# High-part products first behind a norm, and four output tiles over six banks in the gated MLPs

## The chip, the core and the metric

The kernel runs on one core of a Trainium2 chip. The metric is device time in microseconds (us) from the start to the end of one execution; smaller is better. TensorE (PE) multiplies, with its weight loads in a row of their own (PEld); VectorE (DVE), ScalarE (ACT) and GpSimd (POOL) do the elementwise work; SyncE (SP) and ScalarE's queue issue the DMAs. PE adds up its products in eight banks of PSUM.

## What is computed

Two transformer blocks, one after the other, on 256 latent tokens and 256 context tokens of width 1024. The first block has two layers. Each begins and ends with a gated MLP at half weight behind a modulated norm, and has a mixer between them (gated delta rule in one layer, window attention in the other). The second block has a mixer of three branches, a cross attention and an MLP.

```python
def _modulated_norm(h, gain, shift, scale):
    return _rms_norm(h, gain) * (1.0 + scale) + shift

def _swiglu(h, w1, w2):
    a, b = jnp.split(h @ w1, 2, axis=-1)
    return (jax.nn.silu(a) * b) @ w2

for i in range(DEPTH):                       # 2 layers
    mx = (cond_x @ ada_w[i] + ada_b[i]).reshape(n_batch, 3, 3, 1, d)
...
    x = x + FFN_RESIDUAL * mx[:, 0, 2] * _swiglu(
        _modulated_norm(x, norm_g[i, 0], mx[:, 0, 0], mx[:, 0, 1]), ffn_w1[i, 0], ffn_w2[i, 0])
```

In the second block the norm is plain: the gated convolution begins with `rms_norm(h, norm_mix) @ w_in`, and the last MLP is `jnp.square(jax.nn.relu(u @ w_mlp_up)) @ w_mlp_down` with `u = rms_norm(h, norm_mlp)`.

## The kernel before

**Products.** Everything is kept with features on the partitions. A float32 operand is split into a high part (`hi`, rounded to the multiplier's format) and a low part (`lo`, the rest). The product of a weight tile of 128x128 with a token tile is three matmuls (`three`, L218): weights lo x tokens hi (L220), weights hi x tokens lo (L221), weights hi x tokens hi (L222). There are 512 tokens in the stages of mlp00, norm01 to norm11, and 256 in those behind norm12, norm mix and norm mlp. An output tile of 128 features takes eight depth steps (`KT` = 8), so 24 matmuls, in one bank.

**Weights.** They come in units of eight tiles (512 KB). SP loads a unit into one of three landing buffers and, for unit u, waits first for the low parts of unit u-3 (L2614). ACT makes the high parts in one of four slots, and waits for the landing and until PE has used unit u-4 (`feed_act`, L195). POOL makes the low parts (`feed_pool`, L207). Each engine has its order written out by hand; nothing is scheduled by a tool.

**A norm.** The row sums of the squares go through ACT (L411), DVE (L435) and PE (`spread_pe`, L417). Then, for each of the eight depth steps d, DVE multiplies (L441), ACT makes the high part of the normed tokens (L428, two halves where there are 512 tokens), DVE applies scale and shift again (L447) and POOL makes the low part (L463). DVE starts L447 of step d as soon as ACT has made the high part of d.

**`linear`** (L234) runs all products. The first `first` output tiles go side by side: for each d, PE waits for the low part of step d of the tokens (`ready(d)`), then does the three matmuls of each of these tiles. All other output tiles go one after the other, each through all eight d. Tile n is in bank n % 4, and `freed(n)` is the wait until its bank has been read. The gated MLPs' first half (`up_pe`) and the delta mixer's input (`delta_pe`) have first = 2, `glu_pe` and `mlp2_pe` have first = 4. `FIRST` (L2686) lays the weights out in the same order.

**Behind the products of the gated MLPs.** Even tiles are the gate (ACT's silu, L500), odd ones are multiplied with it by DVE (L515). At the start of each tile n, ACT runs `feed_act` up to the unit `max(n+1, first) + 3` of the stream, and only then waits for tile n.

**Work beside.** The modulation vectors of the later layers are computed while the first three gated MLPs (mlp00, mlp01, mlp10) and the delta mixer run, one block of the matrix `ada_w` (1 MB, into the one buffer `ada_landing`) for every two output tiles. ACT issues the first block's DMA behind the wait for tile 0, and PE uses it behind tile 2:

```python
def ada_beside_pe(k, pe, n, units):
    if n >= 2 and (n - 2) // 2 < len(units):
        (ada_turn_pe if n % 2 else ada_pe)(k, pe, units[(n - 2) // 2])

def ada_beside_act(k, act, n, units):
    if n == 0 and units:
        ada_dma(k, act, units[0])
    if n >= 2 and n % 2 == 0 and (n - 2) // 2 < len(units):
        u = units[(n - 2) // 2]
        ada_act(k, act, u)
        if u != units[-1]:
            ada_dma(k, act, u + 1)
```

`linear` calls `beside(n)` behind tile n; for the `first` tiles it calls it for all of them once they are all done.

Of the kernel before, what the change touches and what calls it, by code (L numbers as in the profile page):

```python
# [7 lines left out]
ACT = mybir.ActivationFunctionType  # L8
ALU = mybir.AluOpType
AX_X = mybir.AxisListType.X  # L10

P = 128
D = 1024
KT = D // P
CTX, LAT = 256, 256
# [215 lines left out]
    return k.WH[:, u % SLOTS, at:at + width], k.WL[:, u % SLOTS, at:at + width]  # L231


def linear(k, pe, st, stream, n_tiles, depth, x, tokens, freed, ready=None, first=1, beside=None):  # L234


    nc = k.nc

    def one(n, d):
        t = d * first + n if n < first else n * depth + d  # L240
        w = tile_parts(k, pe, stream, t)
        mm = three(nc, k.B[n % 4][:, 0:tokens], w, x(d), d == 0, d == depth - 1)
        names = []
        if t % UNIT == UNIT - 1:
            names.append(("unit used", k.F.unit(stream, t)))
        if d == depth - 1:
            names.append((st, "acc", n))
        if names:
            mm.then_inc(*k.PE.mark(*names))

    def begin(n):
        if freed(n) is not None:
            pe.wait_ge(*freed(n))

    for n in range(first):
        begin(n)
    for d in range(depth):
        if ready is not None and ready(d) is not None:
            pe.wait_ge(*ready(d))
        for n in range(first):  # L260
            one(n, d)
    for n in range(first):
        if beside is not None:
            beside(n)
    for n in range(first, n_tiles):
        begin(n)
        for d in range(depth):
            one(n, d)
        if beside is not None:
            beside(n)  # L270
# [205 lines left out]

def up_freed(k, st):
    return lambda n: None if n < 4 else (k.DV.after(st, "raw", (n - 4) // 2) if n % 2 else k.AC.after(st, "silu", (n - 4) // 2))  # L480


def up_pe(k, pe, st, stream, x, tokens, ready, units=(), extra=None):
    def beside(n):
        ada_beside_pe(k, pe, n, units)
        if extra is not None:
            extra(n)
    linear(k, pe, st, stream, 2 * FT, KT, x, tokens, up_freed(k, st), ready, first=2, beside=beside)


def up_act(k, act, st, stream, tokens, hi, units=(), extra=None):
    nc = k.nc
    for n in range(2 * FT):
        p = n // 2
        feed_act(k, act, k.F.ahead(stream, max(n + 1, 2) * KT))
        if n % 2 == 0:
            act.wait_ge(*k.PE.after(st, "acc", n))
            if p >= 2:
                act.wait_ge(*k.DV.after(st, "lo", p - 2))
            nc.scalar.activation(k.sil[:, p % 2, 0:tokens], k.B[n % 4][:, 0:tokens], ACT.Silu).then_inc(*k.AC.mark((st, "silu", p)))  # L500
        else:
            act.wait_ge(*k.DV.after(st, "raw", p))
            nc.scalar.activation(hi(p), k.sil[:, p % 2, 0:tokens], ACT.Copy).then_inc(*k.AC.mark((st, "hi", p)))  # L503
        ada_beside_act(k, act, n, units)
        if extra is not None:
            extra(n)


def up_dve(k, dve, st, tokens, hi, lo, units=(), extra=None):
    nc = k.nc  # L510
    for p in range(FT):
        s = k.sil[:, p % 2, 0:tokens]
        dve.wait_ge(*k.PE.after(st, "acc", 2 * p + 1))
        dve.wait_ge(*k.AC.after(st, "silu", p))
        nc.vector.tensor_tensor(s, s, k.B[(2 * p + 1) % 4][:, 0:tokens], ALU.mult).then_inc(*k.DV.mark((st, "raw", p)))  # L515
        dve.wait_ge(*k.AC.after(st, "hi", p))
        nc.vector.tensor_tensor(lo(p), s, hi(p).bitcast(F32), ALU.subtract).then_inc(*k.DV.mark((st, "lo", p)))  # L517
        for n in (2 * p, 2 * p + 1):
            ada_beside_dve(k, dve, n, units)
        if extra is not None:  # L520
            extra(p)
# [6 lines left out]
def down_freed(k, up, st):  # L528
    def freed(n):
        if n >= 4:  # L530
            return k.DV.after(st, "ev", n - 4)
        return k.DV.after(up, "raw", FT - 2 + n // 2) if n % 2 else k.AC.after(up, "silu", FT - 2 + n // 2)
    return freed


# [61 lines left out]
def delta_pe(k, pe):  # L597

    nc, st = k.nc, "dn"

    def freed(n):
        if n < 4:
            return None
        m = n - 4
        return k.AC.after(st, "abt") if m == 0 else k.DV.after(st, "conv", m - 1) if m <= QKV else k.AC.after(st, "z", m - 1 - QKV)

    def beside(n):
        m = n - 3
        if 0 <= m < 16:
            pe.wait_ge(*k.AC.after(st, "sq", m))  # L610
            for c in range(CHUNKS):
                mm = nc.tensor.matmul(k.B[4][:, m * 4 + c:m * 4 + c + 1], k.sq[:, m % 2, c * P:(c + 1) * P], k.C["ones"][:, 0:1],
                                      start=m == 0 and c == 0, stop=True, skip_group_check=True)
            mm.then_inc(*k.PE.mark((st, "stat", m)))
        ada_beside_pe(k, pe, n, ADA_DELTA)
        if n == 2:
            pe.wait_ge(*k.AC.after(st, "abt"))
            for c in range(CHUNKS):
                mm = nc.tensor.transpose(k.B[5][:, c * 32:(c + 1) * 32], k.abt[0:32, c * P:(c + 1) * P], k.C["ident"][0:32, 0:32])
            mm.then_inc(*k.PE.mark((st, "ab")))  # L620
        if n == 5:
            pe.wait_ge(*k.DV.after(st, "g"))
            for d in range(2):
                g = k.dg["g"][:].rearrange("p (c d h) -> p c d h", d=2, h=8)[:, :, d, :]
                nc.tensor.matmul(k.B[5][:, 128 + d * 32:160 + d * 32], k.C["until"][:, d, :], g, start=True, stop=True)
                mm = nc.tensor.matmul(k.B[5][:, 192 + d * 32:224 + d * 32], k.C["ones"], g, start=True, stop=True)
            mm.then_inc(*k.PE.mark((st, "sums")))
        if n > QKV:
            if n == QKV + 1:
                pe.wait_ge(*k.DV.after(st, "r"))  # L630
            for m in (2 * (n - QKV - 1), 2 * (n - QKV - 1) + 1):
                m = m // 2 + 8 * (m % 2)
                bank = 5 + m // 8
                if m % 8:
                    pe.wait_ge(*k.DV.after(st, "normed", m - 1))
                for c in range(CHUNKS):
                    mm = nc.tensor.transpose(ck(k.B[bank], c), column(k.rr, m * 4 + c).to_broadcast([P, P]), k.C["ident"])
                mm.then_inc(*k.PE.mark((st, "spread", m)))

    linear(k, pe, st, "w_dn", DN_TILES, KT, lambda d: (k.n_hi[:, d, :], k.n_lo[:, d, :]), TOK, freed,  # L640
           lambda d: k.PO.after("norm01", "lo", d), first=2, beside=beside)


def delta_act(k, act):
# [855 lines left out]
def both2(k):  # L1500
    return lambda d: (k.m_hi[:, d, :], k.m_lo[:, d, :])
# [35 lines left out]

def glu_pe(k, pe):
    freed = lambda n: None if n < 4 else k.AC.after("glu", "sig", (n - 4) // 2) if n % 2 else k.DV.after("glu", "ev", (n - 4) // 2)
    linear(k, pe, "glu", "w_glu", 2 * KT, KT, both2(k), LAT, freed, lambda d: k.PO.after("norm mix", "lo", d), first=4)  # L1540


def glu_act(k, act):
# [747 lines left out]

def mlp2_pe(k, pe):
    freed = lambda n: k.DV.after("up2", "square", n - 4) if n >= 4 else None
    linear(k, pe, "up2", "w_mlp_up", 4 * KT, KT, both2(k), LAT, freed, lambda d: k.PO.after("norm mlp", "lo", d), first=4)
    out_pe(k, pe, "down2", "w_mlp_down", 4 * KT, lambda d: (k.mh_hi[:, d, :], k.mh_lo[:, d, :]), LAT,
           lambda n: k.DV.after("down2", "ev", n - 4) if n >= 4 else k.DV.after("up2", "square", 4 * KT - 4 + n),
           lambda d: k.DV.after("up2", "lo", max(d, 4 * KT - 5)) if d == 0 or d > 4 * KT - 5 else None)
# [63 lines left out]
def mlp_pe(k, pe, st, extra=None):  # L2361
    norm, up, down, l, n, tokens, after, units = MLPS[st]
    a = TOK - tokens
    hi, lo = hidden(k, tokens)
    up_pe(k, pe, st, "w_" + up, lambda d: (k.n_hi[:, d, a:TOK], k.n_lo[:, d, a:TOK]), tokens, lambda d: k.PO.after(norm, "lo", d), units, extra)
    out_pe(k, pe, st + " down", "w_" + down, FT, lambda d: (hi(d), lo(d)), tokens, down_freed(k, st, st + " down"), down_ready(k, st), stat=after)


# [290 lines left out]
def build(nc, dram, out, steps, counted):  # L2659
    with ExitStack() as ctx:  # L2660
        k = Kit(nc, ctx, dram, steps, counted)
        with nc.Block() as block:
# [21 lines left out]


FIRST = {"w_dn": 2, "w_dn_out": 4, "w_swa_k": 2, "w_swa_out": 4, "w_glu": 4, "w_k": 2, "w_ssd_out": 4,  # L2686
         "w_mix": 4, "w_xo": 4, "w_mlp_up": 4, "w_up00": 2, "w_up01": 2, "w_up10": 2, "w_up11": 2}


def pack(t, name, w):  # L2690
# [158 lines left out]
```

## Time and profile before

| | |
|---|---|
| median of 3 runs | 3163.7 us (3160.8 to 3165.36) |
| the profiled execution, its own time | 3158.29 us |
| its span, first to last instruction | 3156.2 us |
| PE busy | 2999.3 us, 95% of the span |
| mean granted TensorE clock | 0.970 |

The span and all rows below are of one profiled execution. A row of the timeline gives the start in us from the span's start, the duration, the engine, the source line, the operation, what it writes and reads, and, in brackets, how long the engine sat idle before it and who ended that. Matmuls overlap, so the duration of one is longer than the step from one start to the next.

### The profile page before, as it was taken

The page shows a single profiled execution, that of the slowest core. Times are in us where ns is not written, and L with a number is a line of the kernel's source. Part 1 is how long each engine was busy: PE and PEld are TensorE (multiplying, and loading weights), DVE is VectorE, ACT ScalarE, POOL GpSimd, SP SyncE. Part 2 cuts the span into 40 slices and gives each one's busy share as a digit, 9 for nine tenths or more (in the row PEclk, how much of TensorE's full clock was granted, in tenths as well). Part 3 has the DMA queues.
Part 4 walks back from the last instruction along what each step waited for, and adds up shares of the span by engine and source line. Part 5 has one row for each costly group of instructions (what it writes and reads, how often), then busy time and mean ns, then how long its engine had stood idle before and what let it go on. Part 6 is the DMA issues. An engine that isn't in the chain of part 4 may idle for free.

```text
span 3156.2 us, 47130 instructions
## 1 busy us (share of the span) xinstructions
PE 2999.3 (95%) x19462; PEld 2584.0 (82%) x19462; DVE 1244.8 (39%) x2298; ACT 1248.1 (40%) x2122; POOL 1617.3 (51%) x810
## 2 busy tenths in 40 slices
PE   8999999989999899999999999899999898998899
PEld 5777878779999777777777888589999698997899
DVE  2222135524444422211322114745335776622570
ACT  3222234335555332222322224454445556544453
POOL 4333443344443443344433445168887276596587
PEclk9999999999999999999999999899999899998999
DMA  6544224310000144432454323435545153354255
GB/s 251 176 167 148 94 94 156 109 47 1 1 1 1 47 168 178 161 107 94 142 178 135 105 92 88 82 115 189 185 155 176 45 169 112 108 168 140 94 188 167
DMA packets 96884, 381.45 MB, mean 121 GB/s; under 512 B 10369, under 2 KB 15649, under 8 KB 87201
## 3 DMA queue, kind: packets, MB, share of 16 engines
q1 hardware_dynamic: 87456, 311.33, 30.5%
q10 hardware_dynamic: 9216, 67.11, 6.2%
q8 instruction: 155, 2.54, 0.3%
q14 instruction: 57, 0.46, 0.0%
HBM read 374.21 MB, written 4.19 MB: 120 GB/s over the span
## 4 chain that ended last, share of the span: by engine, by line
PE 85%; DVE 5%; POOL 4%; ACT 3%; issue 1%; DMA 1%; SPq 0%; ACTq 0%; POOLq 0%; DVEq 0%
PE bank L220 23%; PE bank L221 22%; PE bank L222 22%; PE bank L750 5%; PE bank L293 2%; POOL weights_lo L213 2%; PE bank L1388 1%; DVE norm_work L447 1%; PE bank L769 1%; DVE norm_work L441 1%; DVE square_sums L405 1%; ACT dn_xt L1036 1%; PE bank L375 1%; ACT weights_hi L203 0%; PE bank L847 0%
## 5 line engine op out<-in xcount | busy, mean ns | idle before, releaser
L213 POOL TENSOR_TENSOR weights_lo<-weights_landing,weights_hi 128x1024 fp32r<-128x1024 f32 x554 | 1334.8, 2413 | 1192.7 <-ACT weights_hi L203 1191.7
L203 ACT ACTIVATE weights_hi<-weights_landing 128x1024 fp32r<-128x1024 f32 x554 | 586.5, 1060 | 1319.6 <-PE bank L222 1238.6
L220 PE MATMUL bank<-normed_hi,weights_lo 128*128 128x256 f32 (+1 forms) x2864 | 979.6, 342 | 39.5 <-POOL normed_lo L463 23.3
L221 PE MATMUL bank<-normed_lo,weights_hi 128*128 128x256 f32 (+1 forms) x2864 | 963.5, 336 | 0.0
L222 PE MATMUL bank<-normed_hi,weights_hi 128*128 128x256 f32 (+1 forms) x2864 | 962.3, 336 | 0.0
L220 PEld LDWEIGHTS bank<-normed_hi,weights_lo 128*128 128x128 f32 x2864 | 546.3, 191 | 133.2 <-issue 32.3
L222 PEld LDWEIGHTS bank<-normed_hi,weights_hi 128*128 128x128 f32 x2864 | 545.6, 190 | 61.5
L221 PEld LDWEIGHTS bank<-normed_lo,weights_hi 128*128 128x128 f32 x2864 | 546.5, 191 | 56.3
L221 PE MATMUL bank<-hidden_lo,weights_hi 128*128 128x512 f32 (+1 forms) x960 | 329.3, 343 | 0.0
L222 PE MATMUL bank<-hidden_hi,weights_hi 128*128 128x512 f32 (+1 forms) x960 | 329.3, 343 | 0.0
L220 PE MATMUL bank<-hidden_hi,weights_lo 128*128 128x512 f32 (+1 forms) x960 | 329.3, 343 | 0.0
L515 DVE TENSOR_TENSOR silus<-silus,bank 128x512 f32<-128x512 f32 (+1 forms) x88 | 54.7, 621 | 565.1 <-PE bank L222 540.1
L517 DVE TENSOR_TENSOR hidden_lo<-silus,hidden_hi 128x512 fp32r<-128x512 f32 (+1 forms) x88 | 212.5, 2415 | 89.6 <-ACT hidden_hi L503 89.6
L222 PEld LDWEIGHTS bank<-hidden_hi,weights_hi 128*128 128x128 f32 x960 | 180.2, 188 | 24.4
L220 PEld LDWEIGHTS bank<-hidden_hi,weights_lo 128*128 128x128 f32 x960 | 180.2, 188 | 24.2
L221 PEld LDWEIGHTS bank<-hidden_lo,weights_hi 128*128 128x128 f32 x960 | 180.2, 188 | 24.1
L944 POOL TENSOR_TENSOR dn_lm<-dn_at,dn_level 128x512 f32<-128x512 f32 (+1 forms) x96 | 114.8, 1212 | 159.7 <-PE bank L750 159.5
L572 DVE SCALAR_TENSOR_TENSOR residual<-bank,gate,residual 128x256 f32<-128x256 f32 x80 | 35.5, 479 | 376.6 <-PE bank L222 376.6
L463 POOL TENSOR_TENSOR normed_lo<-norm_work,normed_hi 128x512 fp32r<-128x512 f32 (+1 forms) x72 | 76.4, 1065 | 82.6 <-DVE norm_work L447 82.6
L1100 DVE TENSOR_TENSOR dn_y<-dn_y,bank 128x512 f32<-128x512 f32 (+1 forms) x96 | 61.7, 643 | 107.2 <-PE bank L750 96.2
L1522 DVE SCALAR_TENSOR_TENSOR bank<-gl,k_pack,bank 128x255 f32<-128x255 f32 (+14 forms) x210 | 99.3, 473 | 7.4
L750 PE MATMUL bank<-dn_xt,dn_lm 128*128 128x128 f32 x640 | 84.1, 285 | 12.2 <-ACT dn_xt L1036 11.3
(414 smaller groups left out, 3906.0 us busy)
## 6 DMA issues: line engine op xcount, KB each, us to landing
weights_landing<-w_up SPq DMA_DIRECT2D x176, 512.0 KB, 3.5
ada_landing<-w_ada ACTq DMA_DIRECT2D x64, 1024.0 KB, 4.9
weights_landing<-w_down SPq DMA_DIRECT2D x88, 512.0 KB, 3.5
weights_landing<-w_dn SPq DMA_DIRECT2D x33, 512.0 KB, 3.5
weights_landing<-w_mlp_up SPq DMA_DIRECT2D x32, 512.0 KB, 3.5
weights_landing<-w_mlp_down SPq DMA_DIRECT2D x32, 512.0 KB, 3.6
weights_landing<-w_gate SPq DMA_DIRECT2D x24, 512.0 KB, 4.3
weights_landing<-w_xbc SPq DMA_DIRECT2D x24, 512.0 KB, 3.5
```

The source lines that it names most:

```text
L203: k.nc.scalar.activation(k.WH[:, u % SLOTS, :], k.W[:, u % LANDS, :], ACT.Copy).then_inc(*k.AC.mark(("unit hi", u)))
L213: k.nc.gpsimd.tensor_tensor(k.WL[:, u % SLOTS, :], k.W[:, u % LANDS, :], k.WH[:, u % SLOTS, :].bitcast(F32), ALU.subtract).then_inc(*k.PO. ...
L220: nc.tensor.matmul(out, ll, rh, start=start, stop=False, skip_group_check=True)
L221: nc.tensor.matmul(out, lh, rl, start=False, stop=False, skip_group_check=True)
L222: return nc.tensor.matmul(out, lh, rh, start=False, stop=stop, skip_group_check=True)
L293: mm = nc.tensor.matmul(k.B[6][32 * j:32 * j + 32, 0:256], k.cond32[:, u % 4 * 2 + d, :], k.ada[slot][:, (d * 4 + j) * 256:(d * 4 + j + 1) ...
L463: k.nc.gpsimd.tensor_tensor(lo(d), work(d), hi(d).bitcast(F32), ALU.subtract).then_inc(*k.PO.mark((st, "lo", d)))
L517: nc.vector.tensor_tensor(lo(p), s, hi(p).bitcast(F32), ALU.subtract).then_inc(*k.DV.mark((st, "lo", p)))
L750: mm = k.nc.tensor.matmul(ck(bank, c), lhs[:, c, :], rhs[:, c, :], start=True, stop=True)
L944: nc.gpsimd.tensor_tensor(k.lm[d][part], k.at_[d][part], level_mask(k, d, s)[part], ALU.mult).then_inc(*k.PO.mark(("head", i, "lm", s, d)))
L1100: nc.vector.tensor_tensor(y, y, bank, ALU.subtract).then_inc(*k.DV.mark(("head", i, "y", s, d)))
L1522: nc.vector.scalar_tensor_tensor(y[:, a:LAT], x[:, 0:LAT - a], w[:, at, j:j + 1], y[:, a:LAT], ALU.mult, ALU.add).then_inc(*k.DV.mark(("co ...
```

## The change

`linear` gets two parameters. With `high`, each depth step of the tiles side by side is cut in two: PE waits for the **high** part of the tokens (made by ACT) and does for each tile the two matmuls that need only it (L271 and L272 of the new code); then it waits for the low part (made by POOL) and does the third matmul of each tile (`low_part`, L242). With `banks`, tile n is in bank n % banks.

`high` is given behind norm00, norm01, norm02, norm10, norm12, norm mix and norm mlp; norm11 and norm xattn stay as they were. In the four gated MLPs first goes from 2 to 4 and the banks from 4 to 6. The calls of `beside` are not edited.

```diff
-def linear(k, pe, st, stream, n_tiles, depth, x, tokens, freed, ready=None, first=1, beside=None):
+def linear(k, pe, st, stream, n_tiles, depth, x, tokens, freed, ready=None, first=1, beside=None, banks=4, high=None):
...
+    def low_part(n, d):
+        t = d * first + n
+        u, at = k.F.unit(stream, t), t % UNIT * P
+        mm = nc.tensor.matmul(k.B[n][:, 0:tokens], k.WH[:, u % SLOTS, at:at + P], x(d)[1], start=False, stop=d == depth - 1,
+                              skip_group_check=True)
+        done(mm, t, n, d)
...
     for d in range(depth):
+        if high is not None:
+            pe.wait_ge(*high(d))
+            for n in range(first):
+                (wh, wl), (xh, xl) = tile_parts(k, pe, stream, d * first + n), x(d)
+                nc.tensor.matmul(k.B[n][:, 0:tokens], wl, xh, start=d == 0, stop=False, skip_group_check=True)
+                nc.tensor.matmul(k.B[n][:, 0:tokens], wh, xh, start=False, stop=False, skip_group_check=True)
+            pe.wait_ge(*ready(d))
+            for n in range(first):
+                low_part(n, d)
+            continue
...
+UP_BANKS = 6
...
 def up_freed(k, st):
-    return lambda n: None if n < 4 else (k.DV.after(st, "raw", (n - 4) // 2) if n % 2 else k.AC.after(st, "silu", (n - 4) // 2))
...
+    return lambda n: (None if n < UP_BANKS else k.DV.after(st, "raw", (n - UP_BANKS) // 2) if n % 2 else
+                      k.AC.after(st, "silu", (n - UP_BANKS) // 2))
...
-    linear(k, pe, st, stream, 2 * FT, KT, x, tokens, up_freed(k, st), ready, first=2, beside=beside)
+    linear(k, pe, st, stream, 2 * FT, KT, x, tokens, up_freed(k, st), ready, first=4, beside=beside, banks=UP_BANKS, high=high)
...
-        feed_act(k, act, k.F.ahead(stream, max(n + 1, 2) * KT))
+        feed_act(k, act, k.F.ahead(stream, max(n + 1, 4) * KT))
...
     linear(k, pe, st, "w_dn", DN_TILES, KT, lambda d: (k.n_hi[:, d, :], k.n_lo[:, d, :]), TOK, freed,
-           lambda d: k.PO.after("norm01", "lo", d), first=2, beside=beside)
+           lambda d: k.PO.after("norm01", "lo", d), first=2, beside=beside, high=lambda d: k.AC.after("norm01", "hi", d))
```

`glu_pe` and `mlp2_pe` get `high` in the same way, the banks in `up_act`, `up_dve` and `down_freed` follow `UP_BANKS`, and `FIRST` has 4 for the four streams of the MLPs.

**PE at the start of mlp00, before.** The first row is the last of the modulation before the MLP, then the tokens' step d = 0 for output tiles 0 and 1.

```order
L307 MATMUL bank7<-k_cond_pack,ada_pieces_66 128x8 x2
L220 MATMUL bank0<-normed_hi_49,weights_lo 128x512
L221 MATMUL bank0<-normed_lo_50,weights_hi 128x512
L222 MATMUL bank0<-normed_hi_49,weights_hi 128x512
L220 MATMUL bank1<-normed_hi_49,weights_lo 128x512
L221 MATMUL bank1<-normed_lo_50,weights_hi 128x512
L222 MATMUL bank1<-normed_hi_49,weights_hi 128x512
```

The same place, changed:

```order
L271 MATMUL bank0<-normed_hi_49,weights_lo 128x512
L272 MATMUL bank0<-normed_hi_49,weights_hi 128x512
L271 MATMUL bank1<-normed_hi_49,weights_lo 128x512
L272 MATMUL bank1<-normed_hi_49,weights_hi 128x512
...
L271 MATMUL bank3<-normed_hi_49,weights_lo 128x512
L272 MATMUL bank3<-normed_hi_49,weights_hi 128x512
L242 MATMUL bank0<-normed_lo_50,weights_hi 128x512
L242 MATMUL bank1<-normed_lo_50,weights_hi 128x512
```

The second matmul needed the tokens' low part; now eight matmuls stand before the first that does, over four banks.

**PE around the first block of ada_w in mlp00, before**, behind output tile 2 (bank 2) and ahead of tile 3:

```order
L221 MATMUL bank2<-normed_lo_50,weights_hi 128x512
L222 MATMUL bank2<-normed_hi_49,weights_hi 128x512
L293 MATMUL bank6<-ada_landing_65,cond32 32x256 x8
L220 MATMUL bank3<-normed_hi_49,weights_lo 128x512
L221 MATMUL bank3<-normed_lo_50,weights_hi 128x512
```

Changed:

```order
L242 MATMUL bank2<-normed_lo_50,weights_hi 128x512
L242 MATMUL bank3<-normed_lo_50,weights_hi 128x512
L312 MATMUL bank6<-ada_landing_65,cond32 32x256 x8
L220 MATMUL bank4<-normed_hi_49,weights_lo 128x512
L221 MATMUL bank4<-normed_lo_50,weights_hi 128x512
```

The block stood behind the whole of tile 2, 24 matmuls after the end of tiles 0 and 1; it now stands right behind the last matmuls of tiles 0 to 3, and ahead of tile 4.

**ACT at the same place, before** (the tokens' high parts, then units of weights, then the gate of tile 0 and the DMA of the block):

```order
L428 ACTIVATE normed_hi_49<-norm_work_51,mod,scale 128x256 x16
L203 ACTIVATE weights_hi<-weights_landing 128x1024 x3
L500 ACT_TABLE_LOAD
L500 ACTIVATE silus_55<-bank0 128x512
L282 DMA ada_landing_65<-w_ada 128x2048
```

Changed:

```order
L203 ACTIVATE weights_hi<-weights_landing 128x1024 x5
L523 ACT_TABLE_LOAD
L523 ACTIVATE silus_55<-bank0 128x512
L301 DMA ada_landing_65<-w_ada 128x2048
L526 ACTIVATE hidden_hi_52<-silus_55 128x512
```

The DMA keeps its place behind tile 0's wait, with two more units of weights ahead of it.

## Rows read from the trace of the kernel before

**Rows 1.** The page: busy us of PE, share of the span, instructions.
```profile
PE 2999.3 (95%) x19462; PEld 2584.0 (82%) x19462; DVE 1244.8 (39%) x2298; ACT 1248.1 (40%) x2122; POOL 1617.3 (51%) x810
```

**Rows 2.** Waits of PE: us in total, times, longest us.
```profile
PE bank L220 <- POOL normed_lo L463: 23.3, 9, 4.0
...
PE bank L220 <- DVE gl L1556: 5.4, 1, 5.4
...
PE bank L220 <- issue: 4.1, 1, 4.1
...
PE bank L220 <- DVE relu_squares L2330: 2.9, 1, 2.9
```

**Rows 3.** Timeline of norm02 and the start of mlp01.
```profile
1097.13 0.74 DVE L447 TENSOR_SCALAR norm_work<-norm_work,scale,mod 128x256 f32<-128x256 f32 x2
...
1099.27 0.80 PE L220 MATMUL bank<-normed_hi,weights_lo 128*128 128x512 f32 x1 [4.03 <-POOL normed_lo L463]
...
1111.63 7.12 POOL L213 TENSOR_TENSOR weights_lo<-weights_landing,weights_hi 128x1024 fp32r<-128x1024 f32 x3
```

**Rows 4.** Timeline, the same step of norm00 and norm10.
```profile
40.30 0.73 DVE L447 TENSOR_SCALAR norm_work<-norm_work,scale,mod 128x256 f32<-128x256 f32 x2 [1.16 <-ACT normed_hi L428]
...
42.43 0.80 PE L220 MATMUL bank<-normed_hi,weights_lo 128*128 128x512 f32 x1 [3.71 <-POOL normed_lo L463]
...
1503.71 0.73 DVE L447 TENSOR_SCALAR norm_work<-norm_work,scale,mod 128x256 f32<-128x256 f32 x2
...
1505.85 0.80 PE L220 MATMUL bank<-normed_hi,weights_lo 128*128 128x512 f32 x1 [4.02 <-POOL normed_lo L463]
```

**Rows 5.** Stretches (PE): us, busy us (instructions), granted clock, DMA share, GB/s.
```profile
41.90:45.30 3.40, 2.87 (x7) 0.51 0.00 0
...
1120.00:1131.20 11.20, 11.20 (x48) 1.00 0.61 209
2306.40:2311.80 5.40, 5.39 (x25) 0.50 0.38 131
2968.10:2974.00 5.90, 5.83 (x27) 0.50 0.01 1
2982.40:2985.20 2.80, 0.00 (x0) 1.00 0.70 203
```

**Rows 6.** Timeline, first blocks of ada_w on PE in mlp00, mlp01 and mlp10.
```profile
61.21 1.07 PE L293 MATMUL bank<-ada_landing,cond 128*32 128x256 f32 x16
...
1118.91 1.07 PE L293 MATMUL bank<-ada_landing,cond 128*32 128x256 f32 x16
...
1525.52 1.07 PE L293 MATMUL bank<-ada_landing,cond 128*32 128x256 f32 x16
```

**Rows 7.** Tile ada_landing: landing of all 64 DMAs, of those issued at 1113.56, 1120.05.
```profile
DMA to landing us min/median/max: 4.6/4.9/7.8
...
DMA to landing us min/median/max: 4.8/4.8/4.8
...
DMA to landing us min/median/max: 7.5/7.5/7.5
```

**Rows 8.** Timeline, the last low part behind norm01, and PE.
```profile
459.26 1.28 POOL L463 TENSOR_TENSOR normed_lo<-norm_work,normed_hi 128x512 fp32r<-128x512 f32 x1 [0.23 <-DVE norm_work L447]
...
460.60 0.50 PE L220 MATMUL bank<-normed_hi,weights_lo 128*128 128x512 f32 x1
```

**Rows 9.** Timeline, norm12 and the start of mlp11.
```profile
2093.59 0.41 DVE L447 TENSOR_SCALAR norm_work<-norm_work,scale,mod 128x256 f32<-128x256 f32 x1
...
2094.87 0.58 PE L220 MATMUL bank<-normed_hi,weights_lo 128*128 128x256 f32 x1 [2.40 <-POOL normed_lo L463]
...
2104.31 1.28 ACT L500 ACT_TABLE_LOAD   x1
...
2109.94 1.06 ACT L203 ACTIVATE weights_hi<-weights_landing 128x1024 fp32r<-128x1024 f32 x1 [1.60 <-DMA weights_landing<-w_up]
```

**Rows 10.** Timeline, the gated convolution's first tiles.
```profile
2303.15 1.06 ACT L203 ACTIVATE weights_hi<-weights_landing 128x1024 fp32r<-128x1024 f32 x1 [1.75 <-DMA weights_landing<-w_glu]
```

## What the change should do to the time

> **What bounds the kernel now.** I read the page first: PE is busy for 95% of the span [rows 1], so a change pays only where PE stands still or runs at half clock, or where it makes PE do either. Then the waits of PE, sorted by what ended them: 23.3 us in nine waits for the tokens' low parts, 4.1 us of the same kind put down to "issue", 5.4 and 2.9 us for the readers of a bank in the two stages that already had four tiles side by side [rows 2]. Then the timeline around each norm, and the granted clock there. The whole prize of this change is in the first class, some 27 us, of which the part from high to low can go.
>
> **Part 1: the start behind a norm, 512 tokens.** DVE starts L447 of step 0 when the high part of step 0 is made, so its start is the moment at which the changed PE may begin. In mlp01 that is 1097.13, and PE began at 1099.27 [rows 3]: 2.1 us. In mlp00 it is 40.30 against 42.43, in mlp10 1503.71 against 1505.85 [rows 4]: 2.1 us each. The later steps should not hold it: 48 matmuls take 11.2 us [rows 5], 0.233 us each, so a depth step of four tiles is 12 x 0.233 = 2.8 us. The low part of step 7 is ready at 1111.6, when POOL goes on to weights [rows 3]; seven steps after step 0's at 1099.2 make it 1.8 us a step. PE is now the slower one.
>
> The fourth unit of weights is needed at depth step 6 and is made behind the norm's low parts: the first of three at 7.12/3 = 2.4 us from 1111.63 [rows 3], so at 1114.0. PE reaches step 6 at 1097.1 + 72 x 0.233 + the half-clock surcharge of about 2 us = 1115.9. Covered, by 1.9 us.
>
> **Part 2: the clock.** Behind each of these fronts PE runs at half clock at first: 2.9 us in mlp00 (42.43 to 45.3), 5.8 in the last MLP, and 5.4 behind the bank wait in the gated convolution; these are the first, the last and one of the middle of eight such stretches with a mean of 4.3 us [rows 5]. Each costs half of its length: 2.15 us on the mean. Beginning 2.1 us earlier should on the mean let the clock rise 2.1 us earlier; I count no change, with 1.1 us per front as the bound to the bad side (it rises when it did, and the early time is spent at half clock). In mlp00 PE would stand still for only 1.6 us (to 40.3, from 42.43 - 3.71 = 38.7 [rows 4]), so the clock may not fall there: I take half of the surcharge of 1.45 us, 0.7.
>
> **Part 3: the block of ada_w loses its cover.** ACT issues the first block's DMA behind the wait for tile 0; PE's order has the block behind tile 2. Before, tile 0 ended with tile 1 and the whole of tile 2 (24 x 0.233 = 5.6 us) lay between: the DMA issued at 1113.56 took 4.8 us [rows 7], and PE took the block at 1118.91 [rows 6]. That cover had 0.5 us to spare. Now tile 0 ends together with tiles 2 and 3, and nothing lies between. Queued behind the waiting block on PE are tile 4 and all that follows. The DMA landed in 4.8 us there; the next one, issued at 1120.05 while units of weights were still coming in, took 7.5 us [rows 7]. The new one is issued at about 1121.7, beside the tail of the same units; I take 5.9 us, nearer to the lower end because most of those units have landed by then, and keep 4.8 and 7.5 as ends.
>
> The three stages, from the first product to the end of "four tiles and one block":
> - mlp01, before: 1118.91 + 1.0 for the block + 5.7 for tile 3 = 1125.6 (26.3 us from the first product; 22.4 of products, 1.0 of block and 2.15 of clock leave 0.8 lost to later steps). Now: 1097.2 + 96 x 0.233 (22.4) + 2.15 = 1121.75; + 0.15 (issue) + 5.9 + 0.1, then 1.0 for the block = 1128.9. **3.3 us later.**
> - mlp10, before: 1525.52 + 6.7 = 1532.2. Now: 1503.8 + 22.4 + 2.15 = 1528.35, + 7.15 = 1535.5. **3.3 us later.**
> - mlp00, before: 61.21 + 6.7 = 67.9. Now: 40.4 + 22.4 + 0.7 + 0.2 (step 0's low part) = 63.7, + 7.15 = 70.8. **2.9 us later.**
>
> Together 9.5 us; with landings of 4.8 us 6.2, with 7.5 us 14.3.
>
> The Trainium skill ("DMA: Bandwidth & Descriptors", section "Queues, rings and completion order") says that each DMA engine takes turns between the queues that have work. By that alone a 1 MB block beside a 512 KB unit would always be the late one, and the upper end, 14.3 us, would be the term and the sum +18.7 instead of +13.9. The rows show both 4.8 and 7.5 us, so they do not settle it.
>
> **Part 4: the clock behind the new stall.** PE stands still for about 6.1 us in each of the three stages. The trace has two idle stretches of this kind between dense products: 5.4 us in the gated convolution, after which PE ran at 0.50 for 5.4 us, and 2.9 us in the last MLP, where the clock stayed at 1.00 [rows 2, 5]. The new ones are longer than the first, so I let the clock fall in all three, at the mean surcharge: 3 x 2.15 = 6.4 us (bounds: 0, and 3 x 2.7 = 8.1).
>
> On this the Trainium skill ("TensorE: Matmul & The Clock Gate", section "Loop structure matters more than you think") speaks against the change: a wait for a DMA between bursts of products drops the array to half rate. The trace agrees at 5.4 us of idling and not at 2.9. With the rule the term is 6.4 us, without it 0 and the sum +7.5.
>
> **Part 5: the delta mixer.** Here two tiles stay side by side, and tile 2 still covers the block. POOL ended the last low part at 460.54 and PE went on at 460.60 [rows 8]; six matmuls followed (1.4 us + 0.1), now two (0.5). The steps before it have the same pace of POOL. Gain 1.0 us; no less than 0.9, no more than the 2.1 of the other fronts.
>
> **Part 6: the stages with 256 tokens.** In mlp11 PE may begin at 2093.6 instead of 2094.87 [rows 9]: 1.3 us. But the gate of tile 0 stands on ACT behind the eighth unit, which landed at 2109.94 [rows 9] behind POOL's and SP's chain, not PE's; with the 1.06 us of that unit, a table load of 1.28 and the gate itself it frees bank 0 at 2112.3 at the earliest. Six banks let PE do tiles 4 and 5 meanwhile. The gain is the 1.3 us or, where the clock rises when it did, half of that; I take 1.0 (bounds 0.6 and 1.3). In the gated convolution the same chain (eighth unit at 2303.15 [rows 10]) ends PE's wait of 5.4 us, with four banks before and after: PE arrives earlier and waits longer. **0.** The last MLP has this form too, with its wait of 2.9 us [rows 2]: 0, but the wait grows to some 4 us, and if the clock then falls, up to 2.7 us are lost.
>
> **Nothing for the rest.** The number of matmuls and weight loads is the same. Four or six banks gain nothing in the steady part, where 48 matmuls fill 11.2 us without a gap [rows 5]. The down products' first banks are read 15 us before they are needed, or 0.6 us behind tile 42, with tile 43's 5.6 us as cover.
>
> **Sum.** 9.5 + 6.4 - 1.0 - 1.0 = +13.9 us. On the profiled execution: 3158.3 + 13.9 = 3172.2 us. It stands 5.4 us below the median of 3163.7; the sum carries over to the median: **3177.6 us**, 0.4% slower.
>
> **The rivals.**
> - **Faster.** The block's wait costs nothing: the mechanism would be that the DMA lands under PE's products after all. Then the fronts are left: 3 x 2.1, 3 x 0.8 of later steps and 0.7 of clock in mlp00, with 2.0 from parts 5 and 6: -11 us, 3153 us. For it: 27 us of waits of PE [rows 2]. Against: the DMA stands behind tile 0 on ACT in the listing, and tile 0 cannot end before the last depth step. It decides from a DMA time below 1 us; the least of 64 is 4.6 [rows 7]. Chance 0.06.
> - **The stall, but the clock holds and the DMA lands in about 4.8 us.** 6.2 - 2.0 = +4, 3168 us, within what can't be told from no change. For it: the idle stretch of 2.9 us kept the clock, and half of the 64 blocks landed within 4.9 us [rows 7]. Against: 5.0 us of idling is near the 5.4 after which it fell. Chance 0.22.
> - **Slower still.** The second block, issued behind the first one's products, has only tile 4 before it (5.6 us): it waits where its DMA takes more than that (the one of 7.5 us did), about 1 us in each stage, and the last MLP's wait lets the clock fall: 14.3 + 8.1 + 2.7 - 2.0 = +23, 3187 us; the waits of the second blocks are inside this bound, since a stalled clock gives them cover. Chance 0.14.
> - The forecast, 0.58: 3171 to 3183.
>
> **Range and chances.** A measurement of this kernel can tell about 0.2% (6.3 us) from no change. From the cases: faster 0.06; same 0.18 (most of the second rival, and a little of the forecast); slower 0.76. The range reaches down into the second rival and up to the third: 3166 to 3187 us.
>
> **What would show it.** In the changed profile: PE waits for "DMA ada_landing" three times for 5 to 8 us, in mlp00, mlp01 and mlp10, and no other stage has it; PE's wait for normed_lo is gone but for the delta mixer, and in its place stand waits of some 2 us for ACT's normed_hi; the wait for L1556's line grows by 1 us or more; clock 0.50 behind the three stalls. The step most open to error is the clock: where in its course the stalls fall can't be read from the trace of before. I am wrong if the DMA is issued before tile 0 ends, or if PE does other products while it waits.

## The result

| | changed | before, in the same comparison |
|---|---|---|
| median | 3181.5 us (3176.8 to 3185.6) | 3162.8 us (3160.8 to 3165.4) |
| profiled execution | 3176.8 us | 3158.3 us |
| its span, mean clock | 3174.8 us, 0.970 | 3156.2 us, 0.970 |

The ratio is 1.006, with an interval from 1.0045 to 1.0076: 18.8 us slower, 18.5 us on the profiled executions. The forecast was +13.9 us, slower. Direction and mechanism hold, the size is 5 us short.

The page of the changed kernel: the span, and the busy us, share and instructions of each engine. The counts of instructions are those of before [rows 1].

```profile
span 3174.8 us, 47130 instructions
...
PE 3001.1 (95%) x19462; PEld 2585.0 (81%) x19462; DVE 1236.8 (39%) x2298; ACT 1247.3 (39%) x2122; POOL 1616.8 (51%) x810
```

PE is busy for only 1.8 us longer, so most of the difference is standing still. Half clock counts as busy time; what the new waits add of it is about made up for in other stretches, since the mean clock is 0.970 in both profiled executions. The waits of PE in the changed kernel (us in total, times, longest us):

```profile
PE bank L312 <- DMA ada_landing<-w_ada: 23.0, 3, 8.9
...
PE bank L271 <- ACT normed_hi L447: 8.7, 6, 1.9
...
PE bank L220 <- DVE gl L1580: 4.9, 1, 4.9
...
PE bank L220 <- DVE relu_squares L2354: 4.6, 1, 4.6
...
PE bank L220 <- POOL normed_lo L482: 4.0, 1, 4.0
...
PE bank L271 <- issue: 2.0, 1, 2.0
```

Set against [rows 2]: the waits for low parts, 23.3 us in nine and 4.1 us of "issue", have shrunk to one of 4.0 (norm11, which was not changed) and one of 0.3 in the delta mixer. In their place stand 8.7 us for high parts and 2.0 of "issue", the same wait in the delta mixer. So the change took 12.4 us of waiting from the fronts (27.4 less 15.0). A wait that was not there before gives back 23.0 us: three times PE stands before the block of ada_w. Its half-clock tail comes on top.

The timeline of mlp01 in the changed kernel, from the first product to the second block. SPq and ACTq rows are DMA issues; in brackets stands how long the engine was idle before, and for whom.

```profile
1102.38 0.80 PE L271 MATMUL bank<-normed_hi,weights_lo 128*128 128x512 f32 x1 [1.91 <-ACT normed_hi L447]
...
1124.03 2.68 SPq L2640 DMA_DIRECT2D weights_landing<-w_up  x2
...
1126.34 1.10 PE L242 MATMUL bank<-normed_lo,weights_hi 128*128 128x512 f32 x4
...
1127.53 1.06 ACT L203 ACTIVATE weights_hi<-weights_landing 128x1024 fp32r<-128x1024 f32 x1 [3.69 <-PE bank L242]
1127.61 0.33 ACTq L301 DMA_DIRECT2D ada_landing<-w_ada  x1
...
1134.71 1.94 PE L312 MATMUL bank<-ada_landing,cond 128*32 128x256 f32 x16 [7.28 <-DMA ada_landing<-w_ada]
...
1136.71 0.33 ACTq L301 DMA_DIRECT2D ada_landing<-w_ada  x1
...
1143.18 1.07 PE L312 MATMUL bank<-ada_landing,cond 128*32 128x256 f32 x16
```

Before, PE came from tile 2 straight to its block at 1118.91 [rows 6]. Now its last product of the four tiles is in the row of 1126.34. It ends at 1127.44, ACT issues the DMA at 1127.61, and PE's next product is at 1134.71. SP had issued two units of weights at 1124.03 and 1126.38, just ahead of the block, and another followed at 1131.00. The block's 16 matmuls take 1.94 us instead of 1.07: they run at half clock. The second block does not wait.

How long the three first blocks took from issue to landing, in mlp00, mlp01 and mlp10 of the changed kernel:

```profile
DMA to landing us min/median/max: 8.7/8.7/8.7
...
DMA to landing us min/median/max: 7.1/7.1/7.1
...
DMA to landing us min/median/max: 6.5/6.5/6.5
```

Stretches of PE in the changed kernel (us, busy us and instructions, granted clock, DMA share, GB/s): the front of mlp00, the front of mlp01, behind the stalls of mlp00, mlp01 and mlp10, and in the last MLP:

```profile
40.60:43.60 3.00, 2.91 (x11) 1.00 0.00 0
1102.30:1107.60 5.30, 5.22 (x12) 0.50 0.01 3
72.50:76.80 4.30, 4.26 (x22) 0.50 0.32 84
1134.70:1138.40 3.70, 3.69 (x20) 0.50 0.38 83
1547.20:1551.40 4.20, 4.12 (x21) 0.50 0.31 80
3002.10:3005.50 3.40, 3.06 (x14) 0.50 0.75 183
```

The same marks in the two profiled executions give this account, in us:

| stage | forecast | measured |
|---|---|---|
| mlp00 | 2.9 + 2.15 = +5.0 | +7.7 |
| delta mixer | -1.0 | -0.9 |
| mlp01 | 3.3 + 2.15 = +5.4 | +6.6 |
| mlp10 | 3.3 + 2.15 = +5.4 | +6.2 |
| mlp11 | -1.0 | -1.1 |
| gated convolution to the cross attention | 0 | +1.1 |
| last MLP | 0, up to 2.7 lost | +0.9 |
| all others together | 0 | -2.0 |
| sum | +13.9 | +18.5 |

The last three rows before the sum cancel by chance (+1.1, +0.9, -2.0), so the 4.6 us that the forecast lacks stand in the three MLPs with a block.

### The profile page after: what moved, and what is told of

It is laid out like the page before. It is cut to its first block, busy times and chain, and to the rows that moved or that the text cites. A ratio compares the mean times of both kernels' runs of the same rounds, so it can differ in the third digit from the quotient of the medians.

```text
span 3174.8 us, 47130 instructions
## 1 busy us (share of the span) xinstructions
PE 3001.1 (95%) x19462; PEld 2585.0 (81%) x19462; DVE 1236.8 (39%) x2298; ACT 1247.3 (39%) x2122; POOL 1616.8 (51%) x810
## 4 chain that ended last, share of the span: by engine, by line
PE 85%; DVE 5%; POOL 4%; ACT 3%; DMA 2%; issue 1%; SPq 0%; ACTq 0%; POOLq 0%; DVEq 0%
PE bank L220 22%; PE bank L221 21%; PE bank L222 21%; PE bank L774 5%; PE bank L312 2%; POOL weights_lo L213 2%; PE bank L1412 1%; PE bank L793 1%; PE bank L242 1%; PE bank L271 1%; PE bank L272 1%; DVE square_sums L424 1%; DMA ada_landing<-w_ada 1%; DVE norm_work L466 1%; ACT dn_xt L1060 1%
## 5 line engine op out<-in xcount | busy, mean ns | idle before, releaser
L220 PE MATMUL bank<-normed_hi,weights_lo 128*128 128x256 f32 (+1 forms) x2656 | 903.0, 340 | 17.6 <-DVE gl L1580 4.9
L221 PE MATMUL bank<-normed_lo,weights_hi 128*128 128x256 f32 (+1 forms) x2656 | 888.9, 335 | 0.0
L222 PE MATMUL bank<-normed_hi,weights_hi 128*128 128x256 f32 (+1 forms) x2656 | 887.6, 334 | 0.0
L220 PEld LDWEIGHTS bank<-normed_hi,weights_lo 128*128 128x128 f32 x2656 | 503.5, 190 | 101.4 <-issue 29.3
L222 PEld LDWEIGHTS bank<-normed_hi,weights_hi 128*128 128x128 f32 x2656 | 503.1, 189 | 56.1
L221 PEld LDWEIGHTS bank<-normed_lo,weights_hi 128*128 128x128 f32 x2656 | 504.1, 190 | 51.7
L540 DVE TENSOR_TENSOR hidden_lo<-silus,hidden_hi 128x512 fp32r<-128x512 f32 (+1 forms) x88 | 198.2, 2252 | 110.5 <-ACT hidden_hi L526 110.5
```

The lines of the kernel that those rows point to most:

```text
L220: nc.tensor.matmul(out, ll, rh, start=start, stop=False, skip_group_check=True)
L221: nc.tensor.matmul(out, lh, rl, start=False, stop=False, skip_group_check=True)
L222: return nc.tensor.matmul(out, lh, rh, start=False, stop=stop, skip_group_check=True)
```

## The experiments

The theory: the stall exists because the DMA of the first block is issued behind tile 0, and it lasts as long as that DMA. The rivals: four tiles over six banks, or the products with high parts, are themselves the cost; or the DMA is late because of the units of weights beside it, and its place does not matter. "Before" was timed again beside each: 3161.2 us beside the first four, 3162.7 us beside the others.

**Issue the DMA ahead of tile 0.** ACT issues the first block at the head of the stage; PE's order is untouched.

```diff
 def ada_beside_act(k, act, n, units):
-    if n == 0 and units:
+    if n == 0 and units and units is ADA_DELTA:
         ada_dma(k, act, units[0])
...
     nc = k.nc
+    if units:
+        ada_dma(k, act, units[0])
     for n in range(2 * FT):
```

> The changed kernel, with the DMA of the first block of ada_w in each of the three gated MLPs issued by ACT ahead of the weights' high parts and ahead of the wait for tile 0, so that it lands under the four tiles. PE's order is that of the change. My theory (the block's lost cover and the half clock behind it are the whole loss): PE's three waits for this DMA (8.9, 7.3 and 6.7 us) go, and the 5.9 us of clock with them. The second block has only tile 4 before it, so 0 to 2 us of wait may stand there in each stage. 3181.5 - 22.9 - 5.9 + 2 = 3155 us (3151 to 3160), faster than the kernel before by 3 to 11 us. Rival (the order of the products, two and then one matmul to a bank, costs PE its pace): the waits go too, but the time stays above 3165 us, and 96 matmuls of a front take visibly more than 22.4 us at full clock.

Measured: 3164.9 us (3160.4 to 3173.0), ratio to before 1.0008 (0.9998 to 1.0018). That is above the expected range and can't be told from before. Some 15 us are back and the place of the DMA is confirmed as the cause of most of the loss, but the 6 us of gain that were forecast are missing. PE waits no more for the first block, but now for the second. The waits of PE, the timeline of mlp01 on PE and ACT, and a stretch of PE behind the wait, of this kernel:

```profile
PE bank L312 <- DMA ada_landing<-w_ada: 9.7, 3, 3.9
...
1122.79 1.07 PE L312 MATMUL bank<-ada_landing,cond 128*32 128x256 f32 x16
1125.33 0.60 ACT L525 ACTIVATE silus<-bank 128x512 f32<-128x512 f32 x1
1126.75 0.63 ACT L528 ACTIVATE hidden_hi<-silus 128x512 fp32r<-128x512 f32 x1 [0.82 <-DVE silus L540]
1126.76 0.33 ACTq L301 DMA_DIRECT2D ada_landing<-w_ada  x1
...
1132.49 1.07 PE L312 MATMUL bank<-ada_landing,cond 128*32 128x256 f32 x16 [2.86 <-DMA ada_landing<-w_ada]
...
1133.90:1137.20 3.30, 3.30 (x9) 0.50 0.93 328
```

PE does the first block at 1122.79, and the second block's DMA, which only has to wait for that, leaves at 1126.76: 4.0 us later. It stands in ACT's queue behind a unit of weights, the table load and gate of tile 0, and hidden_hi, which waits for DVE. Between the blocks lie tile 4 and nothing else. Three waits of 3.9, 2.9 and 2.9 us and 3.4 us at half clock soon after each use up the gain: 9.7 + 3 x 1.7 = 15 us.

**High parts first, nothing else.** Two tiles side by side and four banks, as before.

```diff
-UP_BANKS = 6
+UP_BANKS = 4
...
-    linear(k, pe, st, stream, 2 * FT, KT, x, tokens, up_freed(k, st), ready, first=4, beside=beside, banks=UP_BANKS, high=high)
+    linear(k, pe, st, stream, 2 * FT, KT, x, tokens, up_freed(k, st), ready, first=2, beside=beside, banks=UP_BANKS, high=high)
...
-        feed_act(k, act, k.F.ahead(stream, max(n + 1, 4) * KT))
+        feed_act(k, act, k.F.ahead(stream, max(n + 1, 2) * KT))
```

> The high parts first, as in the change, but two tiles side by side over four banks in the gated MLPs, as before. My theory: each norm with 512 tokens saves the four matmuls that no longer follow the last low part, 1.0 us as in the delta mixer, and mlp11 0.5 us; no wait for a block of ada_w. 3162.8 - 4.5 = 3158 us (3155 to 3161). Rival (the new order of products costs by itself): no faster than before, above 3165 us.

Measured: 3158.3 us (3153.8 to 3164.2), ratio 0.9991 (0.9978 to 1.0003): the median is as expected, and the interval takes in no change. Each front with 512 tokens begins 2.1 us earlier; mlp00 ends 0.8 us earlier, mlp01 0.9, and mlp10, where half clock held on longer, 0.4. With two tiles PE catches up with POOL in the last depth steps, and what is kept are at best the four matmuls less behind the last low part, 4 x 0.233 = 0.93 us.

**Four tiles and six banks, low parts in their old place.**

```diff
-        if high is not None:
+        if False:
```

> Four tiles over six banks in the gated MLPs, as in the change, but each depth step waits for the low part first and does its three matmuls tile by tile, everywhere. My theory: the waits for the blocks of ada_w stay, 5 to 9 us each, the fronts begin 2.1 us later with 512 tokens and 1.3 with 256. 3181.5 + 3 x 1.5 + 1.0 + 1.0 = 3188 us (3184 to 3192). Rival (high parts first is what costs): faster than the changed kernel, below 3178 us.

Measured: 3182.9 us (3179.6 to 3184.5), ratio 1.006 (1.0045 to 1.0075), 1 us below the expected range. It is as slow as the whole change: without the high parts first, the fronts end later, and the block waits shorter. The waits of PE:

```profile
PE bank L220 <- POOL normed_lo L482: 23.0, 8, 4.0
...
PE bank L312 <- DMA ada_landing<-w_ada: 18.1, 3, 7.2
...
PE bank L220 <- issue: 4.1, 1, 4.1
```

PE waits 12 us longer for the tokens than in the changed kernel (23.0 and 4.1 of "issue", against 8.7, 4.0, 2.0 of "issue" and 0.3), but 4.9 us less for the block, which lands in 4.9, 7.0 and 5.5 us: where the fronts end later, less comes in beside its DMA. The profiled executions, the slowest run of this kernel and the fastest of the changed one, lie 7.7 us apart, the medians 1.3 us. The whole loss against before comes with four tiles side by side.

**Early block, four banks.** The first experiment with `UP_BANKS = 4`.

> The changed kernel with the first block's DMA issued early, as in the run before, and four banks in place of six. My theory: tile 4 now waits until ACT has read tile 0, which stands behind the eighth unit of weights (1.06 us), a table load (1.28) and the gate (0.6): 2.0 to 2.4 us of wait behind the block in each of the three stages, and some 5 us in mlp11, where clock is lost too. 11 us above the run with early block and six banks, about 3166 us. Rival (six banks do nothing): the same time as with six.

Measured: 3170.8 us (3164.9 to 3176.8), ratio 1.0028 (1.0014 to 1.0041): 5.9 us over the first experiment where 11 were expected. The waits of PE, and PE behind the four tiles of mlp01:

```profile
PE bank L220 <- ACT silus L525: 12.5, 4, 6.2
...
1123.81 0.50 PE L220 MATMUL bank<-normed_hi,weights_lo 128*128 128x512 f32 x1 [2.12 <-ACT silus L525]
```

Four banks leave tile 4 without a bank for 2.1 us with 512 tokens and 6.2 us in mlp11, so the two further banks are what saves mlp11. In the other stages the 2.1 us cost nothing net: they lie between the two blocks and cover the second block's DMA, whose waits go down from 9.7 us to one of 1.8. In the two profiled executions four banks make mlp11 some 7 us longer and the three stages with a block 5.3 us shorter; that the medians lie further apart than this stays open.

**The block in the middle of the four tiles.** PE takes the first block behind depth step 4 (`mid`) and the second where the first one stood. ACT issues both ahead of tile 0, and its issue at tile 0 is left to the delta mixer.

```diff
             for n in range(first):
                 low_part(n, d)
+            if mid is not None and d == 4:
+                mid()
             continue
...
-    if n >= 2 and (n - 2) // 2 < len(units):
+    if n >= (2 if units is ADA_DELTA else 4) and (n - 2) // 2 < len(units):
         (ada_turn_pe if n % 2 else ada_pe)(k, pe, units[(n - 2) // 2])
...
+    if units:
+        ada_dma(k, act, units[0])
+        feed_act(k, act, k.F.ahead(stream, 2 * KT))
+        ada_act(k, act, units[0])
+        ada_dma(k, act, units[1])
     for n in range(2 * FT):
```

> The changed kernel with cover for the first two blocks of ada_w of each gated MLP: ACT issues the first block's DMA ahead of the weights, PE multiplies it behind depth step 4 of the four tiles, and ACT issues the second block's DMA right then, some 14 us before PE needs it behind tile 4. My theory (lost cover is the whole loss): no wait for ada_landing in the MLPs and no half clock behind the fronts' ends; each of the three MLPs then ends 2.9 us earlier than in the kernel before, the delta mixer saves 0.9 and mlp11 1.2 us, the last MLP loses up to 2 us by its longer wait. 3161 - 10 = 3151 us (3148 to 3156). Rival (four tiles with high parts first bring nothing of themselves, the gain is taken back elsewhere): within 3 us of the kernel before.

Measured: 3152.5 us (3149.2 to 3159.9), ratio 0.9978 (0.9966 to 0.9991), as expected. PE in mlp01 (and the DMA issue of the second block):

```profile
1107.70 1.07 PE L314 MATMUL bank<-ada_landing,cond 128*32 128x256 f32 x16
1108.84 0.34 ACTq L303 DMA_DIRECT2D ada_landing<-w_ada  x1
...
1122.89 1.07 PE L314 MATMUL bank<-ada_landing,cond 128*32 128x256 f32 x16
```

No wait for ada_landing is left: 14 us lie between issue and use. Against before, mlp00 is 3.7 us faster, mlp01 2.0, mlp10 2.6. This is what the fronts are worth once they cost no cover: 8.3 us, where the faster rival had set 9.4 (three times 2.1 and 0.8, and 0.7).

**Only the cover taken away from the kernel before.** Nothing of the change is in it: the block stands ahead of tile 2 instead of behind it.

```diff
+    if units and units is not ADA_DELTA and n == 1:
+        ada_pe(k, pe, units[0])
-    if n >= 2 and (n - 2) // 2 < len(units):
+    if n >= 2 and not (units is not ADA_DELTA and n == 2) and (n - 2) // 2 < len(units):
```

> The kernel before, with one thing moved: in the three gated MLPs PE takes the first block of ada_w right behind tiles 0 and 1 instead of behind tile 2. Nothing else of the change is in it. My theory: three waits for the block, of 5.1 us each since here the units of weights are issued behind the block and not ahead of it (it landed in 4.8 to 5.0 us in the kernel before), and half clock behind most of them: +15 and +4 to 6 us, 3181 us (3176 to 3184). Rival (the change's loss comes from four tiles or from the new order of the products): well below 3172 us, since neither is here.

Measured: 3181.7 us (3181.4 to 3182.0), ratio 1.0068 (1.0048 to 1.0088), as expected. The same loss as the whole change, by itself. The waits of PE, the stall in mlp01, and the clock behind it:

```profile
PE bank L293 <- DMA ada_landing<-w_ada: 16.2, 3, 5.9
...
1124.59 1.93 PE L293 MATMUL bank<-ada_landing,cond 128*32 128x256 f32 x16 [5.07 <-DMA ada_landing<-w_ada]
...
1124.50:1129.60 5.10, 5.01 (x23) 0.50 0.64 250
```

That the loss equals that of the whole change is a coincidence of size: it has no gain at the fronts, and shorter waits. Here the DMAs land in 5.7, 4.8 and 5.0 us, each with a unit of weights issued 0.3 to 0.5 us behind it. From the first product of the front on, the three stages are 8.6, 7.5 and 7.1 us longer: the wait (5.9, 5.1, 5.2) and 1.9 to 2.7 us more, mostly half clock. So my 5.9 us is more than enough for a DMA without units just ahead of it, and the changed kernel's landings are longer for another reason.

**The units of weights held back.** The changed kernel, but SP issues the ninth unit of each of the three streams only when PE is through with the first block.

```diff
         if u >= LANDS:
             sp.wait_ge(*k.PO.after("unit lo", u - LANDS))
+        if u in held:
+            sp.wait_ge(*k.PE.after("ada acc", held[u]))
         sp.dma_start(k.W[:, u % LANDS, :], F.source[u]).then_inc(k.landed[u % LANDS], 16)
```

> The changed kernel with SP's loads from the ninth unit of each of the three MLPs' weights on held back until PE has used the first block of ada_w. My theory (the block's DMA took 8.7, 7.1 and 6.5 us because units of weights were under way ahead of it and beside it): it lands in about 4.8 us in all three, PE's waits fall from 22.9 to about 15.5 us in total, and 3181.5 - 7.5 = 3174 us. Rival (a DMA on ACT's queue is slow after the queue's long rest): landings as before, and no gain.

Measured: 3175.5 us (3170.5 to 3178.2), ratio 1.0045 (1.0027 to 1.0063): 6 us below the changed kernel where 7.5 were expected. The waits, the block of mlp01 and the landing of its DMA:

```profile
PE bank L312 <- DMA ada_landing<-w_ada: 15.3, 3, 5.2
...
1131.21 1.93 PE L312 MATMUL bank<-ada_landing,cond 128*32 128x256 f32 x16 [5.00 <-DMA ada_landing<-w_ada]
...
DMA to landing us min/median/max: 4.8/4.8/4.8
```

With the units gone the block lands in 5.0, 4.8 and 4.9 us instead of 8.7, 7.1 and 6.5. PE's waits fall by 7.7 us, which covers the 4.7 that the forecast lacked (it had allowed 5.9 us for a landing). A queue that is slow after a rest is ruled out with it. The rest, a stall of 5 us and the fallen clock, stays: the place of the issue is the first cause, the units beside it the second.

**Six banks in the gated convolution and the last MLP too**, on top of the block in the middle.

```diff
-    freed = lambda n: None if n < 4 else k.AC.after("glu", "sig", (n - 4) // 2) if n % 2 else k.DV.after("glu", "ev", (n - 4) // 2)
+    freed = lambda n: None if n < 6 else k.AC.after("glu", "sig", (n - 6) // 2) if n % 2 else k.DV.after("glu", "ev", (n - 6) // 2)
...
-    freed = lambda n: k.DV.after("up2", "square", n - 4) if n >= 4 else None
+    freed = lambda n: k.DV.after("up2", "square", n - 6) if n >= 6 else None
```

`banks=6` goes to both calls of `linear`, and the readers of the banks take n % 6.

> The run with the block in the middle, and six banks also in the gated convolution and the last MLP's first half. My theory: there the first reader of a bank stands behind the eighth unit's landing, and PE's waits of 5 and 4.6 us for it shrink by the 5.6 us that tiles 4 and 5 take, with the half clock behind them (2.7 and 1.7 us): 9 to 13 us less than the run with the block in the middle, about 3140 us. Rival (what is saved there is waited for at the next unit, since POOL and the landings set the pace): no more than 4 us less.

Measured: 3136.8 us (3134.4 to 3138.9), ratio to before 0.9928 (0.9904 to 0.9952), 15.7 us below the version with the block in the middle, where 9 to 13 were expected. With four banks PE stood still for 6.1 and 4.6 us in that version; here the waits for gl and relu_squares are gone, and these are stretches of PE in the gated convolution and the last MLP:

```profile
2290.00:2297.00 7.00, 7.00 (x62) 1.00 0.63 213
...
2970.00:2975.00 5.00, 5.00 (x45) 1.00 0.46 156
```

PE does tiles 4 and 5 where it used to wait, and the clock does not fall behind: 7.7 us in the convolution and 6.2 us in the last MLP, more than the waits by the half clock behind them. This kernel beats both, by 26 us against before and 45 against the change.

## Why the prediction was right, and where it was short

- **Part 1, the fronts: right.** PE's first product comes 2.1 us earlier against its surroundings in all three (mlp00 at 40.67, forecast 40.4). The four tiles of mlp00 end at 63.60, forecast 63.7; in mlp01 and mlp10 they take 25.05 and 24.9 us from the first product, forecast 24.55. The difference is the clock.
- **Part 2, the clock of the fronts: near, in part by luck.** mlp01's front ran for 5.3 us at half clock where the mean of 4.3 was taken. In mlp00 the clock did not fall at all, where half a surcharge was set. But behind the same 1.60 us of idling it fell there in the profile with the units held back, and PE ran at 0.50 for 6.1 us.
- **Part 3, the block: right in kind, too small. This is the term that was mis-sized.** PE waits three times for ada_landing and nowhere else, as told. The term took a landing of 5.9 us, "nearer to the lower end because most of those units have landed by then". They had not. In mlp01 and mlp10 two units left in the 3.6 us ahead of the block and another 3.4 us behind it; in mlp00 one left 2.3 us ahead and one 0.1 us behind. Landings were 8.7, 7.1 and 6.5 us, with a mean of 7.4, and mlp00's is above the upper end of 7.5. The waits add up to 23.0 us where 18.3 were forecast (three of 6.1): 4.7 us, as much as the sum lacks. The Trainium skill ("DMA: Bandwidth & Descriptors", section "Queues, rings and completion order"), by which each engine takes turns between the queues that have work, gave +18.7; the measured +18.5 and the landings of 5.0 us or less once the units are held back agree with it. The nearness of the sum is in part luck: the 7.5 us put to it was one landing of before, and mlp10's was 6.5. That a block beside a unit is always the late one does not hold here: six times, in the kernel before and in the one that lost only the cover, a unit was issued 0.3 to 0.5 us behind a first block. The block landed in 4.8 to 5.7 us, and the unit took 5.6 to 6.1 instead of some 3.5. The late blocks were those with units just ahead of them, and the one with a unit 0.1 us behind.
- **Part 4, the clock behind the stalls: right.** It fell in all three, for 4.3, 3.7 and 4.2 us with PE at work: about half of that, 6 us, was lost, forecast 6.4. The rule of the Trainium skill ("TensorE: Matmul & The Clock Gate", section "Loop structure matters more than you think") holds here: behind idle stretches of 4.6 to 8.9 us PE ran at 0.50 each time. The length of the wait alone does not decide below that. The 2.9 us after which the clock stayed at 1.00 were no bound: it fell soon after two waits of 2.9 us in the first experiment and at two of the three waits of 2.1 us in the fourth, whose last MLP kept it behind 3.6 us. What decides there is open.
- **Part 5, the delta mixer: right.** 0.9 us of gain, forecast 1.0; the high-part experiment shows that it is the four matmuls.
- **Part 6: mlp11 right** (1.1 us, forecast 1.0). In the last MLP the wait grew from 2.9 to 4.6 us and the clock fell behind it, the bound that was named; it cost 0.9 us net, and up to 2.7 were allowed for. The convolution's wait did not grow, as "what would show it" had it: 4.9 us against 5.4. It goes with the clock of that front: 6.0 us at half clock in the changed kernel and 3.3 before. With 3.3 us and the block in the middle it was 6.1, with 3.1 us in the high-part experiment 6.2, so at the same clock it does grow, by 0.7 to 0.8 us. Why the stretch to the cross attention is 1.1 us longer I did not settle.
- **The other signs.** The three waits were told as 5 to 8 us, and mlp00's was 8.9. The wait for normed_lo that is left is norm11's, which the forecast had passed over, and not the delta mixer's (0.3 us).
- **The faster rival** is refuted as a description of this kernel, but its number was sound: with the block placed so that it costs nothing the kernel reached 3152.5 us, forecast 3153.
- **The rival that the second block waits** did not come true here, since the first stall gives it 6.5 us of cover (issued 1136.71, used 1143.18). It did in the first experiment.

Not settled: how much the high parts first bring beside four tiles, between 1.3 us by the medians and 7.7 by two profiled executions, of 12 us less waiting. The longer wait for the block takes back 4.9 of them. By the stages of these two it is 5.7 us, with nothing in mlp00 and 2.3 in mlp10.

## What to carry over

When tiles are put side by side, list what was issued behind the first tile and used behind a later one: those transfers lose their cover in one stroke, and a reordering on PE has then to move the DMA issue on the other engine too. Price such a transfer with what the other queues issue just before it, not with its median. And where PE waits for the first reader of a bank, two more banks are worth more than an earlier start: here 15.7 us.

## What the runs showed of the hardware

- A 1 MB block landed in 4.8 to 5.0 us with the other queue held, and in 6.5 to 8.7 us with 512 KB units issued just ahead of it and beside it. With one unit issued 0.3 to 0.5 us behind it, it took 4.8 to 5.7 us, and the unit 5.6 to 6.1. The two units ahead of it in mlp01 themselves took 4.1 and 4.5 us.
- A stall costs more than its length: behind each of twelve idle stretches of 5.0 to 8.9 us before a block, in four kernels, its 16 matmuls took 1.93 us instead of 1.07, and PE ran at clock 0.50 for 3.1 to 6.2 us, half of it lost. Shorter ones go either way: the clock stayed at 1.00 behind 2.9 us [rows 2, 5] and behind 3.6 (last MLP, early block with four banks), and fell soon after 2.9 (early block) and 2.1 (mlp01, early block with four banks).
- A DMA that ACT issues is as late as what stands before it on ACT: 4.0 us, by a unit of weights, a table load, a gate and a wait for DVE that had nothing to do with it.
